# Routing of a mixture-of-experts block: squares summed to token columns, one group choice for all token blocks, four wide products for the counts

## The reference, cut to what matters

```
n2 = rmsnorm(h, norm2_g) * (1 + sc2) + sh2             # 512 x 1024
gp = softmax(n2 @ w_grp + b_grp)                       # 512 x 8 groups
g_p, g_idx = top_k(gp, 1)                              # the best group of a token
el = (n2 @ w_er + b_er).reshape(t, 8, 8)               # 8 experts in each group
e_p, e_loc = top_k(softmax(el[g_idx]), 2)              # the best two of that group
e_glob = g_idx * 8 + e_loc
counts = bincount(e_glob)                              # tokens of each expert
pos    = place of each assignment in the list that is sorted by expert
out    = sum over the two choices of weight * expert(n2)   # 64 experts, w1, w3, w2 each
```

## Time and profile before

| | us |
|---|---|
| median of 3 runs | 3046.65 |
| lowest, highest | 3041.8, 3052.45 |
| profiled execution | 3043.51 |
| its span from first to last instruction | 3041.4 |
| PE busy | 2724.7 (90%) |
| DVE busy | 1586.0 (52%) |
| ACT busy | 737.3 (24%) |

### The profile page before, as it was taken

One profiled execution on the slowest core, in us unless ns is written; L12 is line 12 of the kernel. 1 busy time (PEld: TensorE's weight loads), 2 busy tenths in 40 slices (PEclk: granted clock), 3 DMA queues, 4 the chain that ended last, 5 costly groups with the idle time before them and its releaser, 6 DMA issues.

```text
span 3041.4 us, 46020 instructions
## 1 busy us (share of the span) xinstructions
PE 2724.7 (90%) x18154; PEld 1693.4 (56%) x18155; DVE 1586.0 (52%) x2837; ACT 737.3 (24%) x1392; POOL 637.8 (21%) x629
## 2 busy tenths in 40 slices
PE   7998999999988778776788778999899999998998
PEld 3444444677864333333334333766568877755687
DVE  3558599537544343344444346843564548245544
ACT  3118012102121111111111112313353113144420
POOL 1006012324420000000000003220165541203642
PEclk9999999999989899888889889999899999998999
DMA  8347221243349999999999994221003222200030
GB/s 232 109 155 260 83 83 56 83 139 111 126 159 393 426 426 426 424 417 392 426 426 425 422 423 179 100 83 56 1 2 111 83 85 98 84 28 1 24 116 28
DMA packets 118196, 585.71 MB, mean 193 GB/s; under 512 B 8692, under 2 KB 27732, under 8 KB 92388
## 3 DMA queue, kind: packets, MB, share of 16 engines
q1 hardware_dynamic: 115872, 581.58, 48.0%
q0 software_dynamic: 688, 0.65, 0.7%
q10 hardware_dynamic: 1428, 0.40, 0.1%
HBM read 580.34 MB, written 2.27 MB: 192 GB/s over the span
## 4 chain that ended last, share of the span: by engine, by line
PE 76%; DMA 10%; DVE 8%; issue 5%; ACT 1%; SPq 0%; DVEq 0%; ACTq 0%
PE PS L2222 38%; PE PS L1968 24%; PE PS L1031 8%; DMA S<-in_w 7%; PE PS L488 5%; PE PS L1279 1%; DMA ring<-in_w 1%; DVE TAIL L776 1%; DVE TAIL L1707 1%; ACT tri L582 1%; DMA ring<-in_w_ada 1%; DVE RSTD L1663 0%; DVE S L1750 0%; DVE tri L2820 0%; DVE TAIL L2869 0%
## 5 line engine op out<-in xcount | busy, mean ns | idle before, releaser
L2222 PE MATMUL PS<-nT,ring 128*128 128x512 f32 x1248 | 549.9, 598 | 10.3 <-ACT nT L599 3.3
L2222 PEld LDWEIGHTS PS<-nT,ring 128*128 128x128 f32 x1248 | 235.2, 191 | 298.0 <-issue 280.5
L488 PE MATMUL PS<-S,tri 32*128 32x512 f32 x1040 | 204.3, 628 | 33.9 <-ACT tri L582 32.4
L959 POOL TENSOR_SCALAR nT<-xT,AD 128x512 f32<-128x512 f32 x4 | 6.7, 1689 | 983.0 <-DVE xT L701 983.0
L2222 PE MATMUL PS<-ring,SQ 128*32 128x256 f32 x1344 | 119.1, 501 | 95.7 <-issue 95.7
L701 DVE SCALAR_TENSOR_TENSOR xT<-PS,MOD,xT 128x512 f32<-128x512 f32 x136 | 101.6, 750 | 189.2 <-PE PS L488 189.2
L707 DVE TENSOR_TENSOR tri<-TAIL,PS 128x128 f32<-128x128 f32 x65 | 25.7, 395 | 280.3 <-ACT TAIL L577 280.3
L2936 DVE SCALAR_TENSOR_TENSOR S<-S,COL 128x512 f32<-128x512 f32 x240 | 170.9, 782 | 0.0
L2026 DVE TENSOR_TENSOR TAIL<-PAIR,PS 128x256 f32<-128x256 f32 x46 | 19.4, 421 | 281.2 <-PE PS L1968 281.1
L1968 PE MATMUL PS<-S 128*128 128x256 f32 x712 | 165.1, 379 | 0.0
L1968 PE MATMUL PS<-S,ring 128*128 128x256 f32 x696 | 164.5, 381 | 0.0
(11 more groups left out here) (482 smaller groups left out, 4858.1 us busy)
## 6 DMA issues: line engine op xcount, KB each, us to landing
ring<-in_w SPq DMA_DIRECT2D x74, 2048.0 KB, 18.5
S<-in_w SPq DMA_DIRECT2D x74, 2048.0 KB, 20.4
TAIL<-in_w SPq DMA_DIRECT2D x44, 2048.0 KB, 20.5
ring<-in_w_in SPq DMA_DIRECT2D x40, 2048.0 KB, 7.9
ring<-in_w_ada SPq DMA_DIRECT2D x12, 2048.0 KB, 10.3
TAIL<-decay_rows SPq DMA_DIRECT2D x20, 640.0 KB, 5.4
ring<-in_w_ssm_out SPq DMA_DIRECT2D x4, 2048.0 KB, 8.2
ring<-in_cmp_w SPq DMA_DIRECT2D x4, 2048.0 KB, 8.3
```

The lines of the kernel that those rows point to most:

```text
L488: return pe.matmul(bank, YO[WIN * q:WIN * q + WIN, P * side:P * side + P], PLACE[WIN * q:WIN * q + WIN, 0:T], start=alone, stop=alone, ski ...
L2222: return pe.matmul(o, l, r, start=start, stop=stop)
```

## The change

Four things are changed.

- The squares are no longer multiplied by a matrix of ones on the left. The new `norm_columns` takes each of the 4 blocks of 128 columns of the square sum as the stationary side, and one column of ones as the moving side, so that the sums come out as 4 token columns. ACT takes the root of 128 x 4 numbers into `DEN`; the products that turned a row of roots into columns are gone, and so is their step of the semaphore `router_product`.
- The logits of all 4 token blocks are scaled in one instruction and get their bias in a second.
- The group is chosen for all token blocks at once: a maximum over each 8, an equality with it, a product with 8, 7, ..., 1 (`FIRST`, made ahead of time), a maximum of that, and an equality for the one-hot vector. One product picks the expert logits for all token blocks. The group number is made after the expert's indices.
- The placement sums take 5 products with up to 256 columns in place of 14 products with 64 columns.

```diff
-            pe.wait_ge(S("rstd_root"), 3)
-            for t in range(NT):
-                m = mm(PS[:, 7, t:t + 1], RSTD[0:1, P * t:P * t + P], ones[0:1, 0:1], True, True)
-            m.then_inc(S("router_product"), 1)
...
-            for t in range(NT):
-                o = PS[:, 5, NEXP * t:NEXP * t + NEXP]
-                place(o, above[:, :], CNT[:, t, :], t == 0)
-                for s_ in range(t):
-                    place(o, ones[:, :], CNT[:, s_, :], False)
+            place(PS[:, 5, 0:NT * NEXP], above[:, :], CNT, True)
+            for t in range(1, NT):
+                place(v3(PS[:, 5, NEXP * t:NT * NEXP], NEXP), ones[:, :], CNT[:, t - 1, None, :].to_broadcast([P, NT - t, NEXP]), False)
             pe.wait_ge(S("vector_milestone"), AFTER["windows_ready"] + 1)
             nw = NW32[0:NEXP, 0:1].to_broadcast([NEXP, P])
-            for t in range(NT):
-                m = place(PS[:, 5, NEXP * t:NEXP * t + NEXP], nw, above[0:NEXP, 0:NEXP], False, t == NT - 1)
-            m.then_inc(S("router_product"), 1)
+            place(v3(PS[:, 5, 0:NT * NEXP], NEXP), nw, above[0:NEXP, None, 0:NEXP].to_broadcast([NEXP, NT, NEXP]), False, True) \
+                .then_inc(S("router_product"), 1)
...
+                link(dve.tensor_scalar(FIRST, IOF[:, 0:NGRP], -1.0, float(NGRP), ALU.mult, ALU.add))
...
-            dve.wait_ge(S("router_product"), R_SIGMA)
-            dve.reciprocal(RCOL, PS[:, 7, 0:NT]).then_inc(S("vector_milestone"), 1)
+            dve.wait_ge(S("rstd_root"), 3)
+            dve.reciprocal(RCOL, DEN).then_inc(S("vector_milestone"), 1)
             dve.wait_ge(S("vector_milestone"), AFTER["rcol_ready"] + 1)
-            for t in range(NT):
-                link(dve.scalar_tensor_tensor(out=LG[:, t, :], in0=PS[:, 3, 72 * t:72 * t + 72], scalar=RCOL[:, t:t + 1],
-                                              in1=BRC, op0=ALU.mult, op1=ALU.add))
+            dve.wait_ge(S("router_product"), R_TOKENS)
+            link(dve.tensor_tensor(LG, v3(PS[:, 3, 0:288], 72), RCOL[:, :, None].to_broadcast([P, NT, 72]), ALU.mult))
+            link(dve.tensor_tensor(LG, LG, BRC[:, None, :].to_broadcast([P, NT, 72]), ALU.add))
...
-            for t in range(NT):
-                link(dve.max(GV[:, t, :], LG[:, t, 0:NGRP]))
-                link(dve.max_index(GI[:, t, :], GV[:, t, :], LG[:, t, 0:NGRP]))
-            dve.tensor_scalar(NM, GV[:, :, 0], -1.0, None, ALU.mult).then_inc(S("vector_milestone"), 1)
-            link(dve.tensor_copy(GIF, GI[:, :, 0]))
-            link(dve.tensor_tensor(OH, IOF[:, None, 0:NGRP].to_broadcast([P, NT, NGRP]),
-                                   GIF[:, :, None].to_broadcast([P, NT, NGRP]), ALU.is_equal))
-            for t in range(NT):
-                link(dve.tensor_tensor(SELP[:, t], LG[:, t, NGRP:72].rearrange("p (g e) -> p e g", e=EPG),
-                                       OH[:, t, None, :].to_broadcast([P, EPG, NGRP]), ALU.mult))
+            link(dve.tensor_reduce(GTOP, LG[:, :, 0:NGRP], AX_X, ALU.max))
+            link(dve.tensor_tensor(GV, LG[:, :, 0:NGRP], GTOP[:, :, None].to_broadcast([P, NT, NGRP]), ALU.is_equal))
+            link(dve.tensor_tensor(GV, GV, FIRST[:, None, :].to_broadcast([P, NT, NGRP]), ALU.mult))
+            link(dve.tensor_reduce(GBEST, GV, AX_X, ALU.max))
+            dve.tensor_scalar(NM, GTOP, -1.0, None, ALU.mult).then_inc(S("vector_milestone"), 1)
+            link(dve.tensor_tensor(OH, FIRST[:, None, :].to_broadcast([P, NT, NGRP]),
+                                   GBEST[:, :, None].to_broadcast([P, NT, NGRP]), ALU.is_equal))
+            link(dve.tensor_tensor(SELP, LG[:, :, NGRP:72].rearrange("p t (g e) -> p t e g", e=EPG),
+                                   OH[:, :, None, :].to_broadcast([P, NT, EPG, NGRP]), ALU.mult))
...
             link(dve.tensor_copy(EIF, EI[:, :, 0:2]))
+            link(dve.tensor_scalar(GIF, GBEST, -1.0, float(NGRP), ALU.mult, ALU.add))
...
+        def norm_columns(pe, base, bank):
+            pe.wait_ge(S("square_used"), base + KD - 1)
+            for t in range(NT):
+                m = pe.matmul(PS[:, bank, t:t + 1], square_sum(base)[:, P * t:P * t + P], ones[:, 0:1], start=True, stop=True)
+            m.then_inc(S("square_used"), 1)
...
-                    norm_sum(pe, SQ_N2, 4)
+                    norm_columns(pe, SQ_N2, 4)
...
-            root(4, D, 1)
+            act.wait_ge(S("square_used"), sq[0])
+            act.activation(DEN, PS[:, 4, 0:NT], ACT.Sqrt, bias=EPSC[:, 0:1], scale=1.0 / D).then_inc(S("rstd_root"), 1)
+            roots[0] += 1
```

More of the change, by code:

```diff
@@ L80 @@
 ACC = 2
-R_BIAS, R_LOGITS, R_TOKENS, R_SIGMA, R_COUNT, R_POS, R_TABLE = range(1, 8)
+R_BIAS, R_LOGITS, R_TOKENS, R_COUNT, R_POS, R_TABLE = range(1, 7)
 class Chain:
@@ L313, in build @@
         GV, EV = v3(small(32), 8), v3(small(32), 8)
-        GI, EI = v3(small(32, U32), 8), v3(small(32, U32), 8)
+        GTOP, GBEST, FIRST, EI = small(NT), small(NT), small(NGRP), v3(small(32, U32), 8)
         NM, GSUM, GEX, ESEL = small(4), small(4), v3(small(32), 8), v3(small(32), 8)
```

## The result

The kernel after takes 3031.3 us (median of 9 executions, 3022.8 to 3032.8), beside it the kernel before 3043.9 us (9, 3039.3 to 3052.5). The ratio is 0.9955, 95% interval [0.9942, 0.9969], or 13.7 us less (9.4 to 17.7). The forecast was 6.5 less, with "no change" as the likeliest. That 3031.3 still lies at the lower edge of the range of 3031 to 3048 is luck: the edge stood there for the rival in which the clock stays high, and in this profile the clock fell. The profiled execution of after took 3032.8 us, with a span of 3030.8 and a mean granted clock of 0.948.

A forecast was written before the change was run, and what follows sets the result against it. It took the routing's chain of waits to set when expert 3's loads, and so the weight-bound plateau, start. Savings 1.63 + 2.13 + 2.77 = 6.5 us, from 3046.65 to 3040.1 us; range 3031 to 3048.

The forecast's parts named there:

- no change: Outcome of a time within 0.3% (9.1 us) of before: chance 0.60, against faster 0.35 and slower 0.05.
- the rival in which the clock stays high: PE's clock doesn't fall in the routing's shortened idle time: saving 10.9 us, 3035.7; chance 0.25.
- Parts A to C: Routing: squares to columns saves 1.63 us, group choice 2.13 net, placement sums 2.77; together 6.5.
- its bound: Group choice: the single strided pick, taken at 0.45 us, could cost 1.21 like the four before, losing 0.75.
- The clock falls inside that idle time: Routing before the count: PE idle 874.4 to 879.5, clock falling at 877.4; expected again with idle time about 3.0 us.
- the rival I gave 0.25: PE's clock stays high through the routing: saving 10.9 us, 3035.7; chance 0.25.
- Everything shifts: Behind the placement sums: gather, expert 3's loads and the weight plateau all move earlier by the routing's 6.5 us.
- Part C: Placement sums in the routing: 28 instructions become 10, 7.41 us becomes 4.62 and a hop, saving 2.77.
- The gain doesn't arrive: Loop over experts hides the saving, its plateau held by something other than its start: 3046.6 us; chance 0.11.
- wide forms cost more: Routing's wide instructions cost more than their width: saving only 1.6 us, 3045; chance 0.07.
- Slower by the clock in the loop: Window loop: shifted idle times make PE's clock fall in more windows, 1.69 us each; ten give 3057; chance 0.05.
- Theory P: Formed after the result: PE instruction count ahead of the expert loop places a code block's arrival, the second stop of 2.00 us.

The follow-up runs named there:

- e1: The kernel after, unchanged, run again: 3030.4 us, ratio 0.9945 against before.
- e2: The kernel after with 10 empty products behind PE's wait for w_in, restoring before's instruction count ahead of the loop: 3040.0 us, ratio 1.0004 against before.
- e9: Control: the kernel before with 9 empty products behind the loop over experts: 3045.7 us, ratio 1.0005 against before.
- e14: The kernel before with 9 empty products in PE's pause at about 570 us: 3029.1 us, ratio 0.9957 against before.
- e13: The kernel after with 19 empty products in PE's pause at about 570 us: 3029.7 us, ratio 0.9962 against before.
- e6: The kernel after with 10 empty products ahead of PE's wait for the first w_in slab: 3036.2 us, ratio 0.9973 against before.
- e15: The kernel of e13 run again, unchanged: 3023.4 us, ratio 0.9930 against before.
- e17: The kernel of e13 with 52 linked DVE operations added in the routing: 3055.2 us, ratio 1.0030 against before.
- e11: The kernel after with the 14 narrow placement products put back: 3038.5 us, ratio 0.9976 against before.
- e16: The kernel of e13 with 26 linked DVE operations added in the routing: 3044.0 us, ratio 0.9987 against before.
- e4: The kernel before with 9 empty products behind PE's wait for w_in: 3033.8 us, ratio 0.9965 against before.
- e5: The kernel before with 9 empty products ahead of PE's wait for the first w_in slab: 3032.7 us, ratio 0.9955 against before.
- e10: The kernel before with only the placement sums changed to 5 wide products: 3032.1 us, ratio 0.9949 against before.
- e7: The kernel after with 19 empty products ahead of PE's wait for the first w_in slab: 3032.9 us, ratio 0.9952 against before.
- e3: The kernel after with 19 empty products behind PE's wait for w_in: 3038.6 us, ratio 0.9981 against before.

## Why the forecast was wrong

By stages, in profiled executions (start of routing: last block of `xT`):

| | start | routing | loop | rest |
|---|---|---|---|---|
| before | 863.6 | 53.3 | 944.4 | 1180.0 |
| after | 867.4 | 47.6 | 941.3 | 1174.5 |
| e1 (after) | 866.7 | 46.1 | 941.0 | 1176.5 |
| e2 (stop back) | 867.8 | 46.3 | 944.5 | 1176.9 |
| e9 (before) | 867.6 | 53.3 | 950.3 | 1174.5 |
| e14 (no stop) | 863.2 | 52.8 | 940.2 | 1178.2 |
| e13 (no stop) | 864.6 | 44.5 | 939.8 | 1178.0 |

- **Parts A to C** came out at 1.61, 1.9 and 2.67 us against 1.63, 2.13 and 2.77. `SELP` cost 0.18 more than assumed, inside its bound, and gather and spreads lost 0.41. "The clock falls inside that idle time" held in after and failed in e6, e13 and e15, where the wide products took 1.98: the rival I gave 0.25 came in three profiles, on the same code of the routing, and was worth 8.8 of the 10.9 us I put on it.
- **"Everything shifts"** held for the routing's delay: e13 and e15 to e17 give about one to one. In the pair of before and after the issue came only 2.0 us earlier and not 6.5, since what lies ahead of the routing, which the change doesn't touch, ran 3.8 us later in that execution.
- **The step that failed is Part C** (and the sum that took it over): it said that 28 instructions become 10 and priced them by their own time. What they did as well was to stand ahead of the loop, whose own time the sum took as unchanged. All three parts together took 40 PE instructions from there, of which Part C took 36, and that moved the loop's first product from 20 to 60 instructions ahead of a block's end. The stop of 2.00 us shrank to 0.35 in the turn shown, and from 17.3 to 3.3 us over the nine jumps. Over the loop's stage the five profiles with it (before, e2, e6, e9, e11) took 944.1 to 950.3 us, mean 946.1; the fourteen without it, or with 0.74 at most at any jump, 939.6 to 941.6, mean 940.7: 5.4 us, and no overlap. That is far less than the stops' sum. Where it arises, the fourth and fifth jumps show, first of before, then of after:

```profile
1314.13 7.54 issue
...
1412.56 7.24 issue
```

```profile
1312.54 7.35 issue
...
1407.29 7.02 issue
```

From the loads' issue (916.98 and 914.98) to the fourth jump it is 397.2 and 397.6 us: the second stops of three turns, longer or shorter, change nothing. Nor do those of the turns behind the fifth jump: from it to the ninth (1767.07 and 1761.86) it is 354.5 and 354.6 us. The weights' arrival sets these turns, by this estimate: 18 matrices of 2048 KB at the 421 GB/s measured are 89.7 us, and the three turns from 1045.40 and 1043.31 on took 89.6 and 89.7 each. From the fourth to the fifth jump it is 98.4 and 94.8. This one turn holds the pause half way through the experts in which PE waits 9.9 (before) and 11.6 us (after) for DVE. Over all profiles it took 97.9 to 102.4 us with the stop (mean 99.2) and 94.1 to 97.0 without (mean 95.4), so 3.8 of the 5.4 us. How the stop gets through in just this turn is open.

- **The rivals.** None of mine was this. "The gain doesn't arrive" fell for the routing with e16 and e17, though for the loop's stops it is what most turns show; "wide forms cost more" by 4.74 us. "Slower by the clock in the loop" didn't come: the clock in the loop went the other way, as the stretch of before and then of after shows.

```profile
950.00:1850.00 900.00, 699.93 (x8708) 342.17 (x8703) 364.38 (x744) 142.53 (x245) 0.00 (x0) 0.87 1.00 421
```

```profile
950.00:1850.00 900.00, 691.53 (x8710) 346.87 (x8700) 366.69 (x750) 145.38 (x249) 0.88 (x1) 0.90 1.00 421
```

- **The sum.** Routing 5.7 to 7.2 by the profiles of after and e1, and 5.4 for the loop: 11 to 13 of 13.7 us (interval 9.4 to 17.7). The split isn't settled by the medians. The medians give the stop more than the profiles do: kernels with long routing and no second stop (e4, e5, e14) have a mean ratio of 0.9959, some 12 us below before, where the loop's stage shows 5.4. They also give the routing less (the mean of after, e1, e13, e15 is 0.9948, some 3 us below those). Part of it may be the stretch behind the loop: by the spans it took 1174.6 to 1183.2 us (mean 1178.5) in the five profiles with the stop and 1162.1 to 1178.3 (mean 1173.6) in the others. The same kernel twice differs by 13 us there; whether the stop has a hand in it stays open, with one profile for each run.
- **Theory P is shown**: the stop comes and goes with the count of PE instructions ahead of the loop, on either routing (e2, e6, e11 with it; e4, e5, e10, e14 without, or with a rest of it), not with the same products behind it (e9). That it is a block's arrival shows in the trace as well, which has each packet of the instruction queue. These are its lines for 1054.00 to 1054.10 us of before and for 1051.55 to 1051.65 of after (packets, MB, share of 16 engines):

```profile
q8 instruction: 1, 0.02, 67.1%
```

```profile
q8 instruction: 1, 0.02, 68.7%
```

The shares say that the packets took 1.07 and 1.10 us. Before, PE had stopped at 1054.47 and went on at 1056.47, 1.3 us after the packet's end; after, it had stopped at 1053.71 and went on at 1054.06, 1.4 after it. In nine profiles 80 jumps have a second stop that can be seen, of 0.10 to 2.36 us, and at each PE goes on 1.2 to 1.6 us after the end of such a packet.

- The 3 to 7 packets more (167 to 171 against 164) aren't this block, which comes without the stop too. Each of them stands within 1.2 us of PE's last product before a jump, or beside the packet that the jump itself waits for; where it stands beside it (three jumps of e9, one each of e6 and e11), the first stop took 8.6 to 9.0 us. Why they come only in these kernels is open.

Best of all is the kernel of e13 and e15, the change with 19 empty products in a pause: 0.9962 and 0.9930 against before. Over the kernel after (0.9955, 0.9945) that isn't a resolved gain.

## What to carry over

Where a kernel has a loop with a long body, look at the first pieces behind its jump in the chain of waits: a second "issue" a few instructions in says that the body begins just ahead of a block's end, and a few dozen instructions more or less ahead of the loop move it. Then ask in which turns the engine is what the program waits for: 14 us of stops went, and the loop became some 5 us shorter. Price an edit that changes an engine's instruction count ahead of such a loop by that too, and test any gain of a few per mille with a control that changes the count alone. A stage's gain that shows in the last add of a profile and not in a median calls for a larger delay in the same place, not for a repeat.

## What the runs showed of the hardware

- The jump back at a turn's start cost PE 7.0 to 7.9 us at 166 of the 171 jumps in the 19 profiles, and 8.6 to 9.0 at the other five (e6, e9, e11).
- A second stop, where there was one, ended 1.2 to 1.6 us after a packet of 16.4 KB of the instruction queue had landed (80 jumps in nine profiles).
- PE's empty products (ones times one column) took 5.00 us for 19, 0.26 each, in e7, and 8.27, 0.44 each, in e3.
- A product over 128 x 256 whose operand steps by group within expert took 0.62 us on DVE (`SELP`), plain ones of that size 0.43.
- Wide products: 256, 192, 128, 64 and 256 columns in 3.70 us at a granted clock of 0.50 and in 1.98 at 1.00 (e6), where the 14 narrow ones took 6.37 at 0.50.
